# The opening of a one-core transformer kernel: loads by need, two tiles per pass, squares later, the norm by token

## The chip, the core and the metric

The kernel runs on one core of one Trainium2 chip. The metric is the device time of that core in microseconds (us). A core has TensorE (PE, matrix products into the eight banks of PSUM), VectorE (DVE), ScalarE (ACT), GpSimd (POOL), and SyncE (SP), which only issues transfers here. The engines run beside each other and wait for one another at semaphores; transfers run on 16 DMA engines, fed from the queues of SP, ACT and POOL.

## The reference, cut to what matters

The reference computes two transformer blocks over 512 tokens of width 1024: a recurrent layer with its feed-forward layer, an attention layer with its own, then a second block with retention, window attention and experts. The opening is the first norm and the first product of the recurrent layer:

```python
def rmsnorm(x, g):
    y = xf * lax.rsqrt(jnp.mean(xf * xf, axis=-1, keepdims=True) + EPS)
    return (y * g.astype(jnp.float32)).astype(x.dtype)

def rglru_mixer(h, w_in, conv_w, conv_b, ...):      # h is the normed input
    u = h @ w_in                                    # 1024 -> 2 x 1536
    xb, yb = u[..., :D_RNN], u[..., D_RNN:]
    y = jax.nn.gelu(yb)
    xc = conv over 4 tokens of xb, per channel, + conv_b
    r, i = sigmoid(gates of xc in blocks of 96)     # then a scan over the tokens
```

## The kernel before, in words

Activations lie turned: features on the 128 partitions, the 512 tokens along the free side. `h` holds x in eight tiles of 128 features (two tiles are one load, called x 0 to x 3 below). A product in full precision is made of three in a faster format: each operand is split into a high part (ScalarE rounds it: `a_hi`, `hn_hi`) and a rest (VectorE subtracts: `a_lo`, `hn_lo`), and `three` (L644 to L646) multiplies high by high, high by rest, rest by high. A tile of output is eight steps over the features, 24 matmuls. The norm's factor per token is applied behind the product, since it is the same for all features: the gain is multiplied into `hn_hi` and `hn_lo` at once, and VectorE multiplies the product by `rn`, the inverse root of the mean square, spread over all partitions.

Weights come as panels of 128 by 2048 (1 MB) into two buffers, `a_raw[0]` and `a_raw[1]`; each panel holds two tiles' weights for all eight steps, the two alternating step by step. Panels in the list `HALVES` are rounded in two halves of 1024 columns, so that a product can start with the first four steps.

The order of the work is written out by hand, for each engine:

- Transfers before: SP issues x 0 and panel 0, waits for x 2 (L562), and issues panels 1 to 3 as buffers come free. ACT's queue issues the first constants, x 1, x 2, x 3, the small tables `sm` and the other constants (L1521 to L1525).
- ScalarE before: rounds two tiles of x and squares them, twice; rounds panel 0 in halves; rounds the other four tiles, squaring one; rounds panel 1; takes the root (`root_wide`, L1512) of the sum; then the decay constants (Exp, Ln).
- GpSimd (L3079) adds squares 0 to 4 in four additions. VectorE makes squares 5 to 7, adds them, and adds GpSimd's sum (L2141): the sum of squares.
- TensorE before: 12 calls of `keep` (24 filler matmuls), then tile 0 of panel 0 over eight steps, tile 1 over five, `sums` (a product with a matrix of ones, which sums over the partitions and spreads the result over all of them, L734), the other three steps, and the two tiles of panel 1.
- VectorE before: after panel 1's rest the inverse of 128 by 512 numbers (L2117), then per group of three channel tiles: `take` (product times `rn`, L2207), `conv` (four taps, L2223 and L2226), `low_xc` (the rest of the convolved tile, L2234).
- `rnn_gates` (L792, L799, L800) multiplies the convolved tiles with the gates' weights, panel 2. It waits for the rests of tiles one and two, and later for the third. The gates' sigmoids, decays, the scan and the products of the next panels follow, in the same manner for four groups.

`token_sums` is there before and used in a late stage: it gives the sum of squares by token on the partitions, one column per 128 tokens, by a product whose moving side is one column.

Of the kernel before, what the change touches and what calls it, by code (L numbers as in the profile page):

```python
# [14 lines left out]
P = 128  # L15
# [95 lines left out]
HALVES = [A_RNN, A_K + 2, A_K + 4, A_K + 6, A_VCMP, A_W1V + 1, A_Q]  # L111
# [87 lines left out]
def build(nc, x_t, p_t, w_p, w_a, w_b, w_m, small, const, rope, decay, distance, out_t):  # L199
    ctx = ExitStack()  # L200
    with ctx:
# [331 lines left out]
        def _(sp):  # L533
# [25 lines left out]
            def load_x(i):  # L559
                sp.dma_start(h[:, 2 * i:2 * i + 2, :], x_t.rearrange("(k p) s -> p k s", p=P)[:, 2 * i:2 * i + 2, :]) \  # L560
                  .then_inc(x_loaded[i], 16)

            load_x(0)
            load_a(A_RNN)
            sp.wait_ge(x_loaded[2], 16)
            for u in range(1, 4):
                load_a(A_RNN + u)
# [68 lines left out]
        def _(pe):  # L636
# [99 lines left out]
            def token_sums(t):  # L736

                pe.wait_ge(sq_total, 3 * t + 3)
                for j in range(NT):
                    mm = pe.matmul(bank[4][:, j:j + 1], sq[:, 1, j * P:(j + 1) * P], ones[:, 0:1], start=True, stop=True)  # L740
                mm.then_inc(stat_mm, 1)
# [20 lines left out]
            def hh_first(k):  # L762
                rest(A_RNN, A_RNN, k)
                pe.wait_ge(hn_ready, KT * N_MIX0 + k + 1)
                return hh(k)

            def branch(g, panel, j, b, free, first=False):

                n = A_RNN + 4 * g + panel
                if j == 0:  # L770
                    whole(n, n)
                if g or panel == 3:
                    pe.wait_ge(tile_free, free)
                product(bank[b][:, :], n, j * P, 2 * P, P, hh_first if first else hh, hl).then_inc(tile_ready, 1)

            def rnn_gates(g):

                n = A_RNN + 4 * g + 2
                if g == 0:
                    keep(7, 3)  # L780
# [22 lines left out]
                pe.wait_ge(xc_ready, 3 * g + 2)  # L803
                for q in range(2):
                    own(0, q, True, False)
                pe.wait_ge(xb_taken, g + 1)
# [37 lines left out]
            keep(0, 12)  # L844
            for g in range(RNN_GROUPS):
                f = 8 * g - 3
                branch(g, 0, 0, 0, f, first=g == 0)
                if g:
                    branch(g, 0, 1, 1, f + 1)
                else:  # L850
                    product(bank[1][:, :], A_RNN, P, 2 * P, P, hh, hl, kt=5, last=False)
                    sums(T_MIX0, hs[:, 0, :])
                    product(bank[1][:, :], A_RNN, 5 * 2 * P + P, 2 * P, P, lambda k: hh(k + 5), lambda k: hl(k + 5), kt=3,
                            first=False).then_inc(tile_ready, 1)
                branch(g, 1, 0, 2, f + 2)
                branch(g, 1, 1, 3, f + 3)
                if g:
                    rnn_down(g - 1, 0, 4 if g < RNN_GROUPS - 1 else 2)
# [616 lines left out]
        def _(act):  # L1475
            step = Steps(act, act_step)

            def high_a(s, i=0):
# [4 lines left out]
                if s in HALVES:  # L1483
                    act.activation(a_hi[s % 2][:, 0:WB], a_raw[s % 2][:, 0:WB], ACT.Copy).then_inc(half_rounded, 1)
                    act.activation(a_hi[s % 2][:, WB:WA], a_raw[s % 2][:, WB:WA], ACT.Copy).then_inc(a_rounded, 1)
# [17 lines left out]
            def stat_wait(t):  # L1503
                act.wait_ge(stat_mm, t + 1 + (KT if t > T_KV else 0))
# [17 lines left out]
            for i in (1, 2, 3):  # L1522
                act.dma_start(h[:, 2 * i:2 * i + 2, :], x_v[:, 2 * i:2 * i + 2, :]).then_inc(x_loaded[i], 16)
            act.dma_start(sm[:, :], small).then_inc(params, 16)
            act.dma_start(cn[:, N_FIRST:N_CONST], const[:, N_FIRST:N_CONST]).then_inc(params, 16)  # L1525
            act.wait_ge(consts, 16)
            act.activation(warm[:, 0:1], eps, ACT.Sqrt)
            for i in range(2):
# [5 lines left out]
            high_a(A_RNN)  # L1534
            for m in range(4, KT):
                act.wait_ge(x_loaded[m // 2], 16)
                high_h(m, gain_of(0, m))
                if m == 4:
                    square(T_MIX0, m, h[:, m, :])
            high_a(A_RNN + 1)  # L1540
            root_wide(T_MIX0)


            act.wait_ge(params, 32)
# [3 lines left out]
            act.wait_ge(small_in, 1)  # L1548
            act.activation(spt[:, 3, :], spt[:, 2, :], ACT.Ln).then_inc(small_out, 1)
# [50 lines left out]
            for g in range(RNN_GROUPS + 1):  # L1600
# [23 lines left out]
                if g < RNN_GROUPS:  # L1624
                    high_xc(g, 0)
                    if g == 0:
                        high_a(A_RNN + 2)
# [99 lines left out]
            for m in range(KT):  # L1727
                if m < KT - 1:
                    act.wait_ge(stat_mm, T_KV + 1 + m + 1)
# [339 lines left out]
        def _(dve):  # L2069
            step = Steps(dve, dve_step)  # L2070
            V = dve

            def low_a(s, i=0):
                n = s + 2 * i
                if s in HALVES:
                    V.wait_ge(half_rounded, HALVES.index(s) + 1)
                    V.tensor_tensor(a_lo[s % 2][:, 0:WB], a_raw[s % 2][:, 0:WB], a_hi[s % 2][:, 0:WB], ALU.subtract) \  # L2077
                     .then_inc(half_ready, 1)
                    V.wait_ge(a_rounded, n + 1)
                    V.tensor_tensor(a_lo[s % 2][:, WB:WA], a_raw[s % 2][:, WB:WA], a_hi[s % 2][:, WB:WA], ALU.subtract) \  # L2080
                     .then_inc(a_ready, 1)
# [1330 lines left out]
```

## Time and profile before

| | |
|---|---|
| median of 3 runs | 2160.03 us (2158.39 to 2160.51) |
| the profiled execution | 2158.7 us, span 2156.9 us |
| PE busy | 2104.0 us, 98% of the span |
| DVE, ACT, POOL busy | 59%, 39%, 13% |
| granted PE clock, mean | 0.997 |

Times in the rows are from the start of the span. A row of the timeline gives start, duration, engine, line, operation, output and inputs, shape, how many operations were merged (x3), and in brackets the idle time just before it and what ended that. Matmuls overlap, so their starts tell more than their durations.

### The profile page before, as it was taken

The page shows a single profiled execution, that of the slowest core. Times are in us where ns is not written, and L with a number is a line of the kernel's source. Part 1 is how long each engine was busy: PE and PEld are TensorE (multiplying, and loading weights), DVE is VectorE, ACT ScalarE, POOL GpSimd, SP SyncE. Part 2 cuts the span into 40 slices and gives each one's busy share as a digit, 9 for nine tenths or more (in the row PEclk, how much of TensorE's full clock was granted, in tenths as well). Part 3 has the DMA queues.
Part 4 walks back from the last instruction along what each step waited for, and adds up shares of the span by engine and source line. Part 5 has one row for each costly group of instructions (what it writes and reads, how often), then busy time and mean ns, then how long its engine had stood idle before and what let it go on. Part 6 is the DMA issues. An engine that isn't in the chain of part 4 may idle for free.

```text
span 2156.9 us, 27242 instructions
## 1 busy us (share of the span) xinstructions
PE 2104.0 (98%) x10492; PEld 1583.7 (73%) x10492; DVE 1270.1 (59%) x1696; ACT 834.1 (39%) x1253; POOL 278.7 (13%) x238
## 2 busy tenths in 40 slices
PE   8999999999999999999999999999999999999998
PEld 6787788888878877888888888877778885333346
DVE  7877865555577678875655555577775454000038
ACT  5556522222253445774422222364542232222243
POOL 2334200000010064000100000020000023222220
PEclk9999999999999999999999999999999999999999
DMA  5322323223214352112332222121122158999951
GB/s 198 105 91 98 117 78 117 88 88 116 79 64 149 128 168 79 42 34 89 130 112 92 88 105 100 68 71 52 68 104 88 69 232 327 418 414 394 395 218 59
DMA packets 62478, 298.13 MB, mean 138 GB/s; under 512 B 14064, under 2 KB 14448, under 8 KB 34310
## 3 DMA queue, kind: packets, MB, share of 16 engines
q1 hardware_dynamic: 41584, 259.54, 31.5%
q0 software_dynamic: 19552, 34.55, 5.2%
q10 hardware_dynamic: 1248, 2.76, 0.3%
q8 instruction: 63, 1.03, 0.2%
q14 instruction: 31, 0.25, 0.0%
HBM read 326.37 MB, written 22.48 MB: 162 GB/s over the span
## 4 chain that ended last, share of the span: by engine, by line
PE 74%; DVE 13%; DMA 5%; ACT 4%; issue 3%; POOL 1%; ACTq 0%; DVEq 0%; POOLq 0%
PE psum L644 20%; PE psum L645 20%; PE psum L646 20%; PE psum L1390 4%; DMA panel<-w_m 4%; PE psum L1414 3%; PE psum L1084 2%; DVE a_lo L2085 2%; PE psum L1059 1%; DMA over_panel<-w_m,over_row 1%; ACT a_hi L1488 1%; DVE xc L2226 1%; DVE hs L2181 1%; ACT wp L1881 1%; DVE rn L2117 0%
## 5 line engine op out<-in xcount | busy, mean ns | idle before, releaser
L644 PE MATMUL psum<-hn_hi,a_hi 128*128 128x512 f32 (+1 forms) x1592 | 626.6, 394 | 4.9 <-DVE a_lo L2077 2.1
L646 PE MATMUL psum<-hn_hi,a_lo 128*128 128x512 f32 (+1 forms) x1592 | 619.1, 389 | 0.0
L645 PE MATMUL psum<-hn_lo,a_hi 128*128 128x512 f32 (+1 forms) x1592 | 618.8, 389 | 0.0
L644 PEld LDWEIGHTS psum<-hn_hi,a_hi 128*128 128x128 f32 (+1 forms) x1592 | 297.3, 187 | 77.3 <-issue 10.0
L646 PEld LDWEIGHTS psum<-hn_hi,a_lo 128*128 128x128 f32 (+1 forms) x1592 | 297.3, 187 | 64.4
L645 PEld LDWEIGHTS psum<-hn_lo,a_hi 128*128 128x128 f32 (+1 forms) x1592 | 297.3, 187 | 64.4 <-issue 2.2
L2085 DVE TENSOR_TENSOR a_lo<-a_raw,a_hi 128x2048 fp32r<-128x2048 f32 (+2 forms) x109 | 249.5, 2289 | 78.1 <-ACT a_hi L1488 77.6
L1488 ACT ACTIVATE a_hi<-a_raw 128x2048 fp32r<-128x2048 f32 (+2 forms) x109 | 203.2, 1866 | 73.2 <-PE psum L646 63.3
L2169 DVE TENSOR_TENSOR h<-h,psum 128x512 f32<-128x512 f32 x176 | 119.4, 687 | 78.4 <-PE psum L646 78.4
L3079 POOL TENSOR_TENSOR sq<-sq 128x512 f32<-128x512 f32 x6 | 9.0, 1504 | 1135.9 <-ACT sq L1501 1135.9
L3006 DVE TENSOR_TENSOR xhid<-xsg,psum 128x256 f32<-128x256 f32 x24 | 10.1, 421 | 232.4 <-ACT xsg L2035 232.4
L644 PE MATMUL psum<-hid_hi,b_hi 128*128 128x512 f32 x352 | 137.3, 390 | 2.2 <-DVE h L2169 2.1
L1658 ACT ACTIVATE sg<-sg 128x512 f32<-128x512 f32 x44 | 27.8, 632 | 286.3 <-DVE sg L2342 286.3
L646 PE MATMUL psum<-hid_hi,b_lo 128*128 128x512 f32 x352 | 137.0, 389 | 0.0
L645 PE MATMUL psum<-hid_lo,b_hi 128*128 128x512 f32 x352 | 137.0, 389 | 0.0
L1390 PE MATMUL psum<-panel,xw 128*64 128x512 f32 x512 | 113.4, 595 | 0.0
L2347 DVE TENSOR_TENSOR hid<-sg,psum 128x512 f32<-128x512 f32 x44 | 30.3, 688 | 113.8 <-PE psum L646 113.6
L1660 ACT ACTIVATE hid_hi<-hid 128x512 fp32r<-128x512 f32 x44 | 27.8, 632 | 177.5 <-DVE hid L2347 177.5
L1495 ACT ACTIVATE b_hi<-b_raw 128x1024 fp32r<-128x1024 f32 x64 | 66.9, 1050 | 59.2 <-PE psum L646 57.0
L1390 PEld LDWEIGHTS psum<-panel,xw 128*64 128x64 f32 x512 | 35.3, 137 | 66.8 <-issue 66.3
L2091 DVE TENSOR_TENSOR b_lo<-b_raw,b_hi 128x1024 fp32r<-128x1024 f32 x64 | 79.8, 1253 | 1.0 <-ACT b_hi L1495 1.0
L644 PEld LDWEIGHTS psum<-hid_hi,b_hi 128*128 128x128 f32 x352 | 66.1, 188 | 17.5 <-issue 2.6
(531 smaller groups left out, 3272.4 us busy)
## 6 DMA issues: line engine op xcount, KB each, us to landing
a_raw<-w_a SPq DMA_DIRECT2D x116, 1024.0 KB, 5.0
panel<-w_m SPq DMA_DIRECT2D x96, 1024.0 KB
b_raw<-w_b SPq DMA_DIRECT2D x64, 512.0 KB, 3.3
q_scratch<-q_hi POOLq DMA_DIRECT2D x7, 384.0 KB
q_scratch<-qb_lo POOLq DMA_DIRECT2D x7, 384.0 KB
q_hi<-q_scratch POOLq DMA_DIRECT2D x7, 384.0 KB
q_lo<-q_scratch POOLq DMA_DIRECT2D x7, 384.0 KB
token_rows<-nat POOLq DMA_DIRECT2D x4, 512.0 KB, 5.4
```

The source lines that it names most:

```text
L644: pe.matmul(out, w_hi, x_hi, start=first, stop=False)
L645: pe.matmul(out, w_hi, x_lo, start=False, stop=False)
L646: return pe.matmul(out, w_lo, x_hi, start=False, stop=last)
L1084: mm = pe.matmul(bank[6 + at % 2][side * DV:(side + 1) * DV, t * P:(t + 1) * P], w, x, start=i == 0, stop=i == len(steps) - 1)
L1390: mm = pe.matmul(bank[v][rows, :], xw[:, v, k, rows], w[half][:, k % 4 * 2 * EFF:(k % 4 + 1) * 2 * EFF], start=k == 0, stop=k == KT - 1)
L1414: mm = pe.matmul(bank[4 + 2 * v + hb][rows, :], xturn[:, v, f * P + half * SLOTS:f * P + (half + 1) * SLOTS], w[half][:, f * D + hb * 512: ...
L1488: act.activation(a_hi[s % 2][:, 0:w], a_raw[s % 2][:, 0:w], ACT.Copy).then_inc(a_rounded, 1)
L1495: act.activation(b_hi[s % 2][:, :], b_raw[s % 2][:, :], ACT.Copy).then_inc(b_rounded, 1)
L2085: V.tensor_tensor(a_lo[s % 2][:, 0:w], a_raw[s % 2][:, 0:w], a_hi[s % 2][:, 0:w], ALU.subtract) \
L2091: V.tensor_tensor(b_lo[s % 2][:, :], b_raw[s % 2][:, :], b_hi[s % 2][:, :], ALU.subtract) \
L2169: V.tensor_tensor(h[:, m, :], h[:, m, :], bank[4 + m % 4][:, :], ALU.add).then_inc(y_free, 1)
L2347: V.tensor_tensor(hid[:, f, :], sg[:, f, :], ps[1][:, :], ALU.mult).then_inc(tile_free, 2)
```

## The change

Transfers: panel 0 comes in two halves, the first of them as the first transfer of SP, then x 3 and panel 1; the small tables and the other constants move from ACT's queue to SP's, behind the first rounding; ACT's queue brings the first constants and x 0, x 1, x 2. TensorE makes both tiles of a panel in one pass over the eight steps (`first_tiles`), so that every step's input serves six matmuls at once; panel 1 is now also in `HALVES`. Squares 0 and 1 come after the second half of panel 0, squares 2 to 4 after the first half of panel 1. The norm is taken by token: `token_sums`, a root and an inverse of 128 by 4 numbers, four multiplications of the unit matrix by a column, and a product of ones with the resulting diagonal matrices, which spreads the factor over the partitions; ScalarE copies it to `rn`. Panel 2 is split before the first `take`. The fillers are six calls instead of 12, and the three before the gates go. In group 0 the second `take` comes before the first `low_xc`; in every group the third `take` comes before the second `low_xc`, and the own gates of the first tile wait for that tile alone.

```diff
+            sp.dma_start(a_raw[0][:, 0:WB], first[:, 0:WB]).then_inc(params, 16)
+            sp.dma_start(a_raw[0][:, WB:WA], first[:, WB:WA]).then_inc(a_loaded[0], 16)
+            sp.dma_start(h[:, 6:8, :], ...[:, 6:8, :]).then_inc(x_loaded[3], 16)
+            load_a(A_RNN + 1)
+            sp.wait_ge(half_rounded, 1)
+            sp.dma_start(sm[:, :], small).then_inc(params, 16)
+            sp.dma_start(cn[:, N_FIRST:N_CONST], const[:, N_FIRST:N_CONST]).then_inc(params, 16)
...
+            def first_tiles(panel):
+                s = A_RNN + panel
+                pe.wait_ge(half_ready, HALVES.index(s) + 1)
+                for k in range(KT):
+                    rest(s, s, k)
+                    if panel == 0:
+                        pe.wait_ge(hn_ready, KT * N_MIX0 + k + 1)
+                    for j in range(2):
+                        c = (2 * k + j) * P
+                        mm = three(bank[2 * panel + j][:, :], a_hi[s % 2][:, c:c + P], a_lo[s % 2][:, c:c + P],
+                                   hh(k), hl(k), k == 0, k == KT - 1)
+                        if k == KT - 1:
+                            mm.then_inc(tile_ready, 1)
+                        if panel and k == 2 and j == 0:
+                            pe.wait_ge(consts, 18)
+                            pe.matmul(bank[4][:, :], ones, hs[:, 1, :], start=True, stop=True).then_inc(stat_mm, 1)
+                    if panel and k == 0:
+                        token_sums(T_MIX0, hs[:, 0, :])
...
-            keep(0, 12)
+            keep(0, 6)
...
+            half_a(A_RNN, 0)                      # ScalarE
             for i in range(2):
                 act.wait_ge(x_loaded[i], 16)
                 for m in (2 * i, 2 * i + 1):
                     high_h(m, gain_of(0, m))
+            act.wait_ge(a_loaded[0], 16)
+            half_a(A_RNN, 1)
+            for m in range(2):
+                square(T_MIX0, m, h[:, m, :])
+            for i in range(2, 4):
+                act.wait_ge(x_loaded[i], 16)
                 for m in (2 * i, 2 * i + 1):
-                    square(T_MIX0, m, h[:, m, :])
...
+                    high_h(m, gain_of(0, m))
+            act.wait_ge(a_loaded[1], 16)
+            half_a(A_RNN + 1, 0)
+            for m in range(2, 5):
+                square(T_MIX0, m, h[:, m, :])
+            half_a(A_RNN + 1, 1)
+            root(T_MIX0)
+            high_a(A_RNN + 2)
+            act.wait_ge(stat_mm, 2)
+            act.activation(rn[:, :], bank[4][:, :], ACT.Copy).then_inc(small_out, 1)
...
             for m in range(5, KT):                # VectorE
                 step(V.tensor_tensor(hs[:, m - 5, :], h[:, m, :], h[:, m, :], ALU.mult))
+            half_a(A_RNN + 1, 0)
             for m in range(6, KT):
                 step(V.tensor_tensor(hs[:, 0, :], hs[:, 0, :], hs[:, m - 5, :], ALU.add))
             V.wait_ge(sq_summed, 4)
             V.tensor_tensor(hs[:, 0, :], hs[:, 0, :], sq[:, 0, :], ALU.add).then_inc(sq_total, 3)
-            low_a(A_RNN + 1)
-            inverse_wide(T_MIX0)
+            half_a(A_RNN + 1, 1)
+            inverse(T_MIX0)
+            V.wait_ge(dve_rstd, 1)
+            for j in range(NT):
+                spread = V.tensor_scalar(hs[:, 1, j * P:(j + 1) * P], ident, token[:, 1, j:j + 1], None, ALU.mult)
+            spread.then_inc(consts, 1)
+            low_a(A_RNN + 2)
```

## Rows read from the trace of the kernel before

**Rows 1.** The chain of waits over 0 to 50 us: start, duration, what.
```profile
1.25 7.65 DMA h<-x_t
45.36 0.70 DVE xc_lo L2234
```
**Rows 2.** Timeline of TensorE, from 13 to 97 us.
```profile
13.55 0.50 PE L644 MATMUL psum<-hn_hi,a_hi 128*128 128x512 f32 x1 [1.14 <-DVE a_lo L2077]
...
23.78 1.10 PE L734 MATMUL psum<-hs,cn 128*128 128x512 f32 x2
...
37.69 1.46 PE L640 MATMUL psum<-cn 128*128 128x256 f32 x6
...
46.11 0.49 PE L799 MATMUL psum<-xc_hi,a_hi 64*128 64x512 f32 x1 [0.65 <-DVE xc_lo L2234]
...
95.35 0.50 PE L644 MATMUL psum<-rhid_hi,b_hi 128*128 128x512 f32 x1 [1.99 <-DVE b_lo L2091]
```
**Rows 3.** Timeline of VectorE, from 23 to 40 us.
```profile
23.01 0.69 DVE L2141 TENSOR_TENSOR hs<-hs,sq 128x512 f32<-128x512 f32 x1
...
25.82 3.35 DVE L2117 RECIPROCAL rn<-rn 128x512 f32<-128x512 f32 x1
...
29.42 0.68 DVE L2207 TENSOR_TENSOR xb<-psum,rn 128x512 f32<-128x512 f32 x1
...
30.72 2.32 DVE L2226 SCALAR_TENSOR_TENSOR xc<-xb,sm,xc 128x511 f32<-128x511 f32 x3
...
37.90 2.02 DVE L2085 TENSOR_TENSOR a_lo<-a_raw,a_hi 128x1792 fp32r<-128x1792 f32 x1
```
**Rows 4.** Transfers: 0 to 4.5; 4.2 to 4.6; 4.5 to 7; 9 to 13; SP.
```profile
DMA packets 427, 0.82 MB, mean 183 GB/s; under 512 B 30, under 2 KB 158, under 8 KB 411
...
q1 hardware_dynamic: 53, 0.21, 125.8%
q10 hardware_dynamic: 3, 0.00, 1.2%
...
q1 hardware_dynamic: 108, 0.85, 83.2%
q10 hardware_dynamic: 89, 0.18, 18.8%
...
q10 hardware_dynamic: 650, 1.66, 105.0%
q1 hardware_dynamic: 1, 0.01, 1.4%
...
10.58 0.33 SPq L539 DMA_DIRECT2D a_raw<-w_a  x1
```
**Rows 5.** Timeline of ScalarE, from 8 to 13 us.
```profile
8.92 1.33 ACT L1515 ACTIVATE hn_hi<-h,cn 128x512 fp32r<-128x512 f32 x2 [1.16 <-DMA h<-x_t]
10.16 1.13 ACT L1501 ACTIVATE tmp<-h 128x512 f32<-128x512 f32 x2
11.20 1.04 ACT L1484 ACTIVATE a_hi<-a_raw 128x1024 fp32r<-128x1024 f32 x1
```
**Rows 6.** Timeline of GpSimd and VectorE, from 7 to 16 us.
```profile
7.85 1.26 POOL L3079 TENSOR_TENSOR sq<-sq 128x512 f32<-128x512 f32 x1 [7.38 <-ACT sq L1501]
12.27 1.23 DVE L2077 TENSOR_TENSOR a_lo<-a_raw,a_hi 128x1024 fp32r<-128x1024 f32 x1 [1.18 <-ACT a_hi L1484]
12.36 2.28 POOL L3079 TENSOR_TENSOR sq<-sq,tmp 128x512 f32<-128x512 f32 x1
13.41 2.32 DVE L2080 TENSOR_TENSOR a_lo<-a_raw,a_hi 128x1024 fp32r<-128x1024 f32 x1
```
**Rows 7.** Token sums in a later stage (timeline); narrow multiplications (groups: count, total, mean ns).
```profile
1766.40 0.95 PE L740 MATMUL psum<-cn,sq 128*128 128x1 f32 x8
...
L2684 DVE TENSOR_SCALAR wp<-wp,wst 128x128 f32<-128x128 f32 x8 | 2.2, 281 | 0.0
```
**Rows 8.** TensorE near 1470 us: timeline, and busy times with the granted clock (PEclk).
```profile
1468.92 1.09 PE L1185 MATMUL psum<-cn,wp 128*128 128x128 f32 x8 [3.02 <-DVE wp L2684]
...
1470.00:1472.00 2.00, 2.00 (x7) 1.57 (x6) 2.00 (x3) 1.93 (x2) 0.00 (x0) 0.53 0.00 0
```

More of the change, by code:

```diff
@@ L759, in down, with branch @@
                                 mm.then_inc(y_ready, 1)
[L762 to L767, printed above, removed]
+            def first_tiles(panel):
[16 more added lines that the diff above has]
+                        token_sums(T_MIX0, hs[:, 0, :])
+            def branch(g, panel, j, b, free):
                 n = A_RNN + 4 * g + panel
@@ L771, in branch @@
                     whole(n, n)
-                if g or panel == 3:
-                    pe.wait_ge(tile_free, free)
-                product(bank[b][:, :], n, j * P, 2 * P, P, hh_first if first else hh, hl).then_inc(tile_ready, 1)
+                pe.wait_ge(tile_free, free)
+                product(bank[b][:, :], n, j * P, 2 * P, P, hh, hl).then_inc(tile_ready, 1)
             def rnn_gates(g):
                 n = A_RNN + 4 * g + 2
-                if g == 0:
-                    keep(7, 3)
                 pe.wait_ge(a_ready, n + 1)
@@ L843, in _ @@
             pe.wait_ge(consts, 16)
-            keep(0, 12)
+            keep(0, 6)
             for g in range(RNN_GROUPS):
                 f = 8 * g - 3
-                branch(g, 0, 0, 0, f, first=g == 0)
                 if g:
+                    branch(g, 0, 0, 0, f)
                     branch(g, 0, 1, 1, f + 1)
-                else:
[L851 to L858, printed above, removed]
+                    branch(g, 1, 0, 2, f + 2)
+                    branch(g, 1, 1, 3, f + 3)
+                    rnn_down(g - 1, 0, 4 if g < RNN_GROUPS - 1 else 2)
+                else:
+                    first_tiles(0)
+                    first_tiles(1)
                 if 0 < g < RNN_GROUPS - 1:
@@ L1476, in _, with half_a @@
             step = Steps(act, act_step)
+            def half_a(s, half):
+                c = slice(WB * half, WB * half + WB)
+                act.activation(a_hi[s % 2][:, c], a_raw[s % 2][:, c], ACT.Copy) \
+                   .then_inc(a_rounded if half else half_rounded, 1)
             def high_a(s, i=0):
@@ L1521, in _ @@
             act.dma_start(cn[:, 0:N_FIRST], const[:, 0:N_FIRST]).then_inc(consts, 16)
-            for i in (1, 2, 3):
+            for i in range(3):
                 act.dma_start(h[:, 2 * i:2 * i + 2, :], x_v[:, 2 * i:2 * i + 2, :]).then_inc(x_loaded[i], 16)
-            act.dma_start(sm[:, :], small).then_inc(params, 16)
-            act.dma_start(cn[:, N_FIRST:N_CONST], const[:, N_FIRST:N_CONST]).then_inc(params, 16)
             act.wait_ge(consts, 16)
             act.activation(warm[:, 0:1], eps, ACT.Sqrt)
+            act.wait_ge(params, 16)
+            half_a(A_RNN, 0)
             for i in range(2):
@@ L1531, in _ @@
                     high_h(m, gain_of(0, m))
-                for m in (2 * i, 2 * i + 1):
-                    square(T_MIX0, m, h[:, m, :])
[L1534 to L1544, printed above, removed]
+            act.wait_ge(a_loaded[0], 16)
[4 more added lines that the diff above has]
+                act.wait_ge(x_loaded[i], 16)
+                for m in (2 * i, 2 * i + 1):
+                    high_h(m, gain_of(0, m))
[8 more added lines that the diff above has]
+            act.activation(rn[:, :], bank[4][:, :], ACT.Copy).then_inc(small_out, 1)
+            act.wait_ge(params, 48)
             lam = smc("lam", 0, RNN_TILES)
@@ L2071, in _, with half_a @@
             V = dve
+            def half_a(s, half):
+                c = slice(WB * half, WB * half + WB)
+                if half:
+                    V.wait_ge(a_rounded, s + 1)
+                else:
+                    V.wait_ge(half_rounded, HALVES.index(s) + 1)
+                V.tensor_tensor(a_lo[s % 2][:, c], a_raw[s % 2][:, c], a_hi[s % 2][:, c], ALU.subtract) \
+                 .then_inc(a_ready if half else half_ready, 1)
             def low_a(s, i=0):
@@ L2215, in conv @@
                 if t < 2:
-                    take(g, t)
+                    if n != 1:
+                        take(g, t)
                 else:
@@ L2270, in _ @@
                     conv(g, 0)
+                    if g == 0:
+                        one_more()
+                        take(0, 1)
                 if 0 < g < RNN_GROUPS:
```

68 lines of the change are left out of this document (30 added, 38 removed).

## The prediction

> **What bounds the kernel now.** I read the busy table first: the matrix engine is busy for 98% of the span. Then the waits of that engine, to see where the rest goes, and the chain of waits over the first 75 us, to see which of the opening's waits set the end. The reader is to see three things. The first product starts at 13.55 and the four tiles of the opening end at 37.7, where the filler matmuls begin [rows 2]. The gate products then wait twice for VectorE's xc_lo, the second time until 46.11 [rows 1, 2]. And behind 46.11 the products run until a wait of 1.99 at 95.35, again for VectorE [rows 2]; that chain starts at the gates, since their sigmoids wait for TensorE. So the opening is worth what it brings forward one event, the third xc_lo, which ends at 46.05 (45.36 + 0.69), and all behind it moves with it one for one. Before it lies one unbroken VectorE chain from the sum of squares (23.01 + 0.69 = 23.7): half of a panel's rounding rest, the wide reciprocal 3.35, the take at 29.42, three convolutions with a panel's rest 2.02 between them [rows 3].
>
> That fixes the method: find the end of the sum of squares after the change, add the new way to the take, add the new way to the third xc_lo, and compare with 46.05.
>
> **From the take to the third xc_lo.** Now 46.05 - 29.42 = 16.63. The rest of panel 2 (2.02, L2085) moves ahead of the take. The 0.70 in which VectorE waits for ScalarE's first xc_hi is now filled: the log's addition (0.17, moved) and the second take (0.7) stand there. Sum 16.63 - 2.02 - 0.70 + 0.2 = 14.1. The sample is 3.62 for the first convolution (29.42 to 30.72 + 2.32) [rows 3]. Taking the third tile ahead of low_xc costs nothing: its 0.6 covers the second rounding. The table load for Exp and the one for Ln lie beside convolutions, where ScalarE waits for VectorE. PE's first own gates no longer wait for the second xc_lo, but they are not last: the third is.
>
> **From the sum to the take.** Now 29.42 - 23.7 = 5.7: panel 1's rest 2.1, the wide reciprocal 3.35, two small operations. After: four matmuls by one column, 0.95 [rows 7]; root, high part of panel 2 (1792 wide, about 1.7 by the 1.04 of 1024 [rows 5]) and its rest 2.02, masks 0.15; with the gaps, 5.15. Beside it on TensorE: 0.95, six and three products at 0.23 = 2.05, the spreading product 1.10 [rows 2], the copy 0.7: 4.8, so both ways are about equally long and neither hides much of the other. VectorE's own part (half a rest 1.2, a reciprocal of four columns, four 128-wide multiplies) ends before TensorE reaches the spreading product. The 3.35 is thus mostly paid again: gain 0.55. Behind the waiting spreading product stand 33 products of panel 1 (7.5), due for the third take some 8 us later: no loss.
>
> So the third xc_lo ends at (end of the sum) + 5.15 + 14.1 = sum + 19.25, and the change wins only if the sum ends before 46.05 - 19.25 = 26.8. It could be 3.1 us later than now. The rest is: when does it end?
>
> **Arrivals.** The queues (q1 is SP's, q10 ACT's) have moved 0.82 MB at 4.5 us and then 0.40 MB per us [rows 4]. Two orders are possible when both queues hold work. In order of issue: from 4.2 to 4.6 the SP queue moved 53 packets and the ACT queue 3, though slice 1 of x had been issued there at 1.25 [rows 1, 4], and from 9 to 13 the SP queue moved 1 packet, though panel 1 was issued at 10.58, until the ACT queue was nearly empty [rows 4]. Packet by packet in turn: from 4.5 to 7 it was 108 packets to 89 [rows 4]; these two had been issued together. I take issue order, with turns within a pair issued together. Check on now: constants 0.17, x 0 0.52, panel 0 1.05, x 1 0.52 are 2.27 MB, moved at 8.1; its landing was 8.9 [rows 1, 5], so about 0.75 is added.
> After, pairs as issued: (half panel 0, constants) 0.70 MB, landed 5.0; (other half, x 0) 1.75 MB, 6.8 + 0.75 = 7.5; (x 3, x 1) 2.8 MB, 10.3; (panel 1, x 2) 4.36 MB, 13.4 + 0.75 = 14.1. The small tables follow behind, by 17, and are needed at 31.
> The Trainium skill's DMA: Bandwidth & Descriptors (Queues, rings and completion order) says that an engine takes the queues in turn, packet by packet; by that alone x 1 would land at 12.8 instead of 10.3; it is rival D, which is worked out from the rows.
>
> **ScalarE** (rounding 0.66, square 0.56, half panel 1.0 [rows 5]): half panel from 5.5; x 0 rounded 7.5 to 8.85; x 1 10.3 to 11.65; second half to 12.6; two squares to 13.65; x 2 and x 3 14.1 to 16.6; half of panel 1 to 17.6; squares 2 to 4 end at 18.1, 18.7, 19.2.
> TensorE starts at 9.0 (7.5, a rounding 0.66, a rest 0.7; now 13.55), four steps of 1.37 with hardly a wait to 14.5, waits for x 2 until 15.7, and ends both tiles at 21.2. That is the gain the change is built on: 4.5 us at its start.
>
> **VectorE and GpSimd** decide. GpSimd adds squares: 1.26 with VectorE idle, 2.28 beside a rest of VectorE, whose next rest took 2.32 for 1.23 [rows 6]. Each waits for the other to end: a GpSimd addition holds VectorE up by about 1.1. Now these pairs lie at 12 to 17, before the sum's chain; after, three additions fall into the middle of it, because squares 2 to 4 come last. VectorE: rests of x end at 17.6, then three squares (0.7), the half rest of panel 1 (1.15), two additions (0.7), final addition 0.7, and between them three additions of GpSimd at 1.15: 17.6 + 2.1 + 1.15 + 1.4 + 0.7 + 3.45 = 26.4. Half of panel 1 is ready only at 24.3, so TensorE idles 21.2 to 24.3.
> The Trainium skill's SBUF — State Buffer (SBUF: two separate sides) calls it an exclusive lock on a port pair that the two engines share, taken for a whole operation; this trace agrees with 2.28 and 2.32. It speaks against the change, and by it the sum is at 26.4.
> Without such waits VectorE's own work to 22.6 and GpSimd's three additions, 1.26 each from 18.1 on with what they lose, would let the sum end near 24.1: a rival.
>
> **Sum.** Take at 26.4 + 5.15 = 31.55, third xc_lo at 45.65, against 46.05: 0.4 us gained. The profiled execution took 2158.7 (span 2156.9), so 2158.3 for such a one; the median of the runs, 2160.03, stands 1.3 above it, and I forecast 2160.0 - 0.4 = 2159.6. Removed fillers (six and three calls) stood in idle time and cost nothing.
>
> **Unknown costs and bounds.** The lock: 0 to 3 x 1.1; I take 2.3 net (26.4 against 24.1), nearest to the pair in rows 6. Four diagonal multiplies, not in the trace: the nearest, 128 wide, took 0.28 each [rows 7], so 0 to 1.1 in all; VectorE has 1.3 to spare there, so hidden at either end. x 2: 11.6 (panel 1 held back as from 9 to 13) to 16.6 (below, D); at 11.6 ScalarE's own work becomes the limit and 0.45 is all that is won.
>
> **Rivals.**
> (B) No lock where it matters: the additions of GpSimd fall into VectorE's gaps. Sum 24.1, change 24.1 + 19.25 - 46.05 = -2.7: 2157.3. For it: the first addition took 1.26. Against: VectorE has no gap after 17.6.
> (C) Slower, by TensorE's clock. Place: the idle 21.2 to 24.3. After a wait of 3.02 at 1468.92 the granted clock was 0.53 (the lower level, 1.2 GHz) from 1470 to 1472 [rows 8]. Price: the nine products between the sum and the spreading product take 0.43 instead of 0.23, 1.8 more, and the spreading product up to 1; the path there has 0.35 to spare: +2.5 - 0.4 = +2.1: 2162.1. It decides from a wait near 3 us on; against it, 1.99 at 95.35 [rows 2] did no harm.
> (D) Slower, by turns: a packet of the one queue, then one of the other, as 108 to 89 [rows 4]. Packets are rows: 4 KB of a half panel, 2 KB of x, 8 KB of panel 1. The halves overtake x 0 (landed 8.1), and x 1's last packet moves with panel 1's last, at 3.84 MB, so 12.05 + 0.75 = 12.8. ScalarE reaches squares 2 to 4 at 20.2 to 21.3, the sum ends at 28.3: +1.5: 2161.5. Were the small tables to take turns with x 2 as well, x 2 would land with them, at 5.36 MB: 16.6, which costs 0.4 more, since ScalarE is ready for it at 16.2.
> (E) Much faster: x lands early and no lock, sum near 22.2: -4.6: 2155.4. It needs two of my readings wrong.
>
> **Chances.** Forecast 0.40, B 0.21, C 0.12, D 0.12, E 0.15. A measurement of this kernel tells 0.2% (4.3 us) from nothing. Beyond -4.3 lies E, and not all of it is deeper: 0.13 faster. Beyond +4.3 lie only C and D together, 0.06. So 0.81 within. The range takes in B, C, D and the edge of E: 2155.5 to 2162.8.
>
> **What would show it.** First product near 9 and not 13.5; both tiles of panel 0 ended near 21; a wait of 2 to 3 us before panel 1; GpSimd's last three additions at 1.8 to 2.3 each, between 18 and 23; the sum at 26.4; the copy of the norm at about 31; third xc_lo at 45.6. A granted clock below 1 near 24 would be C; x 1 after 12, D. The forecast fails if the sum ends before 25, or if the first convolution starts before 29.4, and also if the gates' gain is not found again at the wait now at 95.35.

## The result, and the profile after

The changed kernel takes 2163.83 us (median of 21 runs, 2160.96 to 2164.96), the kernel before 2160.01 (21 runs beside them, 2158.37 to 2161.13): a ratio of 1.0017, 95% interval 1.0011 to 1.0023. It is 3.8 us slower; forecast were 0.4 us faster and a range that ended at 2162.8. The profiled execution took 2164.38 us (span 2162.6, mean granted clock 0.996).

TensorE's timeline of the changed kernel:

```profile
15.43 0.50 PE L645 MATMUL psum<-hn_hi,a_hi 128*128 128x512 f32 x1 [1.37 <-DVE hn_lo L2157]
19.26 0.47 PE L645 MATMUL psum<-hn_hi,a_hi 128*128 128x512 f32 x1 [0.81 <-DVE hn_lo L2157]
27.47 0.50 PE L645 MATMUL psum<-hn_hi,a_hi 128*128 128x512 f32 x1 [2.49 <-DVE a_lo L2106]
29.70 1.75 PE L741 MATMUL psum<-cn,hs 128*128 128x1 f32 x8
35.13 1.02 PE L779 MATMUL psum<-hs,cn 128*128 128x512 f32 x2
51.17 0.49 PE L812 MATMUL psum<-xc_hi,a_hi 64*128 64x512 f32 x1 [1.55 <-DVE xc_lo L2277]
...
100.61 0.50 PE L645 MATMUL psum<-rhid_hi,b_hi 128*128 128x512 f32 x1 [1.99 <-DVE b_lo L2123]
```

Set these beside [rows 2]. The last two lines answer to the waits at 46.11 and 95.35: 5.06 and 5.26 later. So the opening's loss is carried on almost one for one, as the method said, and nearly everything is decided before the third xc_lo: the two profiled executions, 2164.38 and 2158.7, differ by 5.7, more than the medians do. Against the kernel before, which waited once for the rests of x, for 1.00, TensorE now waits twice for them, and new is the wait of 2.49 ahead of panel 1.

VectorE's timeline:

```profile
18.31 2.79 DVE L2157 SCALAR_TENSOR_TENSOR hn_lo<-h,cn,hn_hi 128x512 fp32r<-128x512 f32 x4 [0.90 <-ACT hn_hi L1532]
21.02 4.19 DVE L2170 TENSOR_TENSOR hs<-h 128x512 f32<-128x512 f32 x3
25.25 2.17 DVE L2106 TENSOR_TENSOR a_lo<-a_raw,a_hi 128x1024 fp32r<-128x1024 f32 x1
27.34 1.41 DVE L2173 TENSOR_TENSOR hs<-hs 128x512 f32<-128x512 f32 x2
28.83 0.69 DVE L2175 TENSOR_TENSOR hs<-hs,sq 128x512 f32<-128x512 f32 x1
...
31.78 0.18 DVE L2145 RECIPROCAL token<-token 128x4 f32<-128x4 f32 x1 [1.12 <-ACT token L1525]
32.00 0.87 DVE L2181 TENSOR_SCALAR hs<-cn,token 128x128 f32<-128x128 f32 x4
33.37 2.03 DVE L2117 TENSOR_TENSOR a_lo<-a_raw,a_hi 128x1792 fp32r<-128x1792 f32 x1 [0.50 <-ACT a_hi L1505]
36.82 0.23 DVE L2186 CAST masks<-cn 128x128 bf16<-128x128 f32 x1 [1.42 <-ACT rn L1567]
36.96 0.68 DVE L2249 TENSOR_TENSOR xb<-psum,rn 128x512 f32<-128x512 f32 x1
...
50.42 0.69 DVE L2277 TENSOR_TENSOR xc_lo<-xc,xc_hi 128x512 fp32r<-128x512 f32 x1 [0.69 <-ACT xc_hi L1624]
```

The sum of squares ends at 29.52 (28.83 + 0.69); in [rows 3] it was 23.7, forecast were 26.4. The take is at 36.96, 7.44 after it, where 5.15 were forecast. The third xc_lo ends at 51.11, 14.15 after the take, where 14.1 were forecast.

ScalarE's timeline (its waits date the arrivals) and GpSimd's:

```profile
9.25 1.34 ACT L1532 ACTIVATE hn_hi<-h,cn 128x512 fp32r<-128x512 f32 x2 [2.13 <-DMA h<-x_t]
13.87 1.33 ACT L1532 ACTIVATE hn_hi<-h,cn 128x512 fp32r<-128x512 f32 x2 [3.28 <-DMA h<-x_t]
17.55 2.56 ACT L1532 ACTIVATE hn_hi<-h,cn 128x512 fp32r<-128x512 f32 x4 [0.36 <-DMA h<-x_t]
21.66 2.99 POOL L3120 TENSOR_TENSOR sq<-sq,tmp 128x512 f32<-128x512 f32 x2 [3.10 <-ACT tmp L1518]
24.80 1.53 POOL L3120 TENSOR_TENSOR sq<-sq,rstd 128x512 f32<-128x512 f32 x1
```

x 0, x 1 and x 2 arrived at 9.25, 13.87 and 17.55; forecast were 7.5, 10.3 and 14.1. Next, transfers in 0 to 5 us, then by queue in 10 to 11 and 13 to 14 us (packets, MB, share of the engines):

```profile
DMA packets 277, 0.75 MB, mean 151 GB/s; under 512 B 17, under 2 KB 130, under 8 KB 277
...
q1 hardware_dynamic: 39, 0.32, 77.0%
q10 hardware_dynamic: 40, 0.08, 21.8%
...
q1 hardware_dynamic: 78, 0.25, 63.3%
q10 hardware_dynamic: 81, 0.15, 39.8%
```

From 10 to 11 panel 1 (q1, rows of 8 KB) and x 1 (q10, rows of 2 KB) move one packet each in turn, so x gets 0.08 MB per us and panel 1 gets 0.32, though x 1 was issued first. From 13 to 14 the small tables (q1, rows of about 3.3 KB) do the same to x 2. The Trainium skill's DMA: Bandwidth & Descriptors (Queues, rings and completion order) says that each engine takes the queues in turn, a packet at a time; the trace agrees, 39 to 40, where one packet in the profile is one row.

Last, busy times and granted clock (third number from the end) from 26 to 38 us:

```profile
26.00:28.00 2.00, 0.53 (x2) 0.48 (x3) 2.00 (x2) 0.00 (x0) 0.33 (x1) 1.00 0.00 0
28.00:30.00 2.00, 2.00 (x7) 1.36 (x7) 1.88 (x4) 0.00 (x0) 0.00 (x0) 0.52 0.00 0
30.00:32.00 2.00, 2.00 (x9) 1.90 (x10) 0.84 (x3) 0.51 (x2) 0.00 (x0) 0.50 0.43 70
32.00:34.00 2.00, 2.00 (x6) 1.54 (x5) 1.50 (x5) 1.33 (x1) 0.00 (x0) 0.50 0.76 299
34.00:36.00 2.00, 2.00 (x7) 1.27 (x6) 1.40 (x1) 0.00 (x0) 0.00 (x0) 0.77 0.99 408
36.00:38.00 2.00, 2.00 (x10) 1.64 (x9) 1.15 (x3) 1.79 (x3) 0.00 (x0) 1.00 1.06 401
```

After the wait of 2.49 the granted clock is at its lower level (1.2 of 2.4 GHz) until about 35. Exactly there stand the token sums (1.75 us instead of 0.95 [rows 7]) and the products up to the spreading one. Two causes, then, sum up to the 5.06: a sum that is late by 3.1 against the forecast, and 2.3 more between the sum and the take; with the forecast of -0.4 that makes 5.0.

### The profile page after: what moved, and what is told of

It reads as the page before. It is cut to its first block, busy times and chain, and to the rows that moved or that the text cites. A ratio compares the mean times of both kernels' runs of the same rounds, so it can differ in the third digit from the quotient of the medians.

```text
span 2162.6 us, 27236 instructions
## 1 busy us (share of the span) xinstructions
PE 2105.2 (97%) x10482; PEld 1583.1 (73%) x10482; DVE 1269.3 (59%) x1701; ACT 834.6 (39%) x1255; POOL 277.5 (13%) x238
## 3 DMA queue, kind: packets, MB, share of 16 engines
q10 hardware_dynamic: 960, 1.75, 0.2%
## 4 chain that ended last, share of the span: by engine, by line
PE 74%; DVE 12%; DMA 6%; ACT 4%; issue 3%; POOL 1%; ACTq 0%; DVEq 0%; POOLq 0%
PE psum L645 20%; PE psum L646 20%; PE psum L647 20%; PE psum L1401 5%; PE psum L1425 3%; DMA panel<-w_m 3%; PE psum L1095 2%; DVE a_lo L2117 1%; PE psum L1070 1%; DMA over_panel<-w_m,over_row 1%; ACT a_hi L1505 1%; DVE xc L2269 1%; DMA h<-x_t 1%; DVE hs L2223 1%; ACT wp L1907 1%
```

## The experiments

Each kernel was timed in 5 rounds beside the kernel before (medians of that: 2160.23 in the first group of four runs, 2159.22 in the second, 2159.41 in the last three). e1 to e5 are the changed kernel with one edit, e6 is e1 with one, e8 to e11 are e7 with one; where an edit moves arrivals, ScalarE and VectorE follow the new order. "Sum" is the end of the sum of squares, "take" the start of the first take and "third xc_lo" the end of that operation, all in the profiled execution; the kernel before has 23.7, 29.42 and 46.05. "Against before" is the difference of the medians. The ratio is not formed from the medians: for e1 it is 1.0014, by the medians it would be 1.0008.

| kernel | sum | take | third xc_lo | against 46.05 | median | against before | ratio, 95% interval |
|---|---|---|---|---|---|---|---|
| changed kernel | 29.5 | 36.96 | 51.11 | +5.1 | 2163.83 | +3.8 | 1.0011 to 1.0023 |
| e1 fillers | 29.5 | 34.65 | 48.81 | +2.8 | 2161.89 | +1.7 | 1.0005 to 1.0023 |
| e2 panel 1 held | 26.9 | 32.77 | 46.92 | +0.9 | 2160.93 | +0.7 | 0.9997 to 1.0015 |
| e3 squares early | 28.7 | 33.90 | 48.06 | +2.0 | 2161.58 | +1.4 | 0.9999 to 1.0017 |
| e4 old transfers | 25.9 | 32.38 | 46.54 | +0.5 | 2160.41 | +0.2 | 0.9994 to 1.0012 |
| e5 VectorE adds | 28.7 | 35.27 | 49.40 | +3.4 | 2163.12 | +3.9 | 1.0008 to 1.0026 |
| e6 e1, wide norm | 29.8 | 37.35 | 51.50 | +5.5 | 2164.98 | +5.8 | 1.0015 to 1.0034 |
| e7 winner | 21.1 | 26.99 | 41.13 | -4.9 | 2154.64 | -4.6 | 0.9965 to 0.9983 |
| e8 e7, GpSimd adds | 20.9 | 26.77 | 40.92 | -5.1 | 2153.64 | -5.6 | 0.9960 to 0.9982 |
| e9 e7, new transfers | 25.6 | 31.44 | 45.59 | -0.5 | 2158.67 | -0.7 | 0.9988 to 1.0006 |
| e10 e7, panel 0 halved | 21.0 | 26.81 | 40.96 | -5.1 | 2153.91 | -5.5 | 0.9961 to 0.9983 |
| e11 e7, wide norm | 20.2 | 28.38 | 42.51 | -3.5 | 2155.37 | -4.0 | 0.9972 to 0.9990 |

In all twelve the take is followed by the third xc_lo's end after 14.13 to 14.16 us, and the fifth column and the seventh differ by at most 1.3 us. Read from one execution each, this event ranks the kernels as the medians do, but for e5 and the changed kernel, which change places. Where the two columns part, a conclusion below goes no further than what both say.

**e1: fillers before panel 1** (does the clock cost 2.3?).

```diff
                 s = A_RNN + panel
+                if panel:
+                    keep(5, 6)
                 pe.wait_ge(half_ready, HALVES.index(s) + 1)
```

> The changed kernel with six filler calls put where TensorE waits for panel 1's first half (24.98 to 27.47 in its trace). Theory C (the wait, 2.5 us behind two shorter ones, lets the clock fall, and the products between the sum and the spreading product run at half speed): the granted clock stays at 1.00 from 28 to 36, the token sums take 0.95 and not 1.75, the copy of the norm starts near 34.0 instead of 36.19, the third xc_lo ends near 48.9 instead of 51.1, and the time is 2.0 to 2.3 below the changed kernel's median of 2163.8, so near 2161.6; single runs scatter less than its 2161.0 to 2165.0. Rival (the low clock has another cause, or is not on the path): clock and times as they are, 2163.8.

The granted clock was 1.00 in every slice from 20 to 36, and at the same sum (29.54) the take came 2.3 earlier. The two lines of TensorE, token sums and spreading product:

```profile
29.59 1.05 PE L741 MATMUL psum<-cn,hs 128*128 128x1 f32 x8 [0.45 <-DVE hs L2177]
32.66 1.02 PE L781 MATMUL psum<-hs,cn 128*128 128x512 f32 x2
```

From token sums to spreading product it was 3.07 us instead of 5.43. So theory C is shown, and its size on the path, 2.3, by one trace of each kernel. The times bear it out less sharply: the medians differ by 1.9 (2163.83 and 2161.89), but the intervals of the two ratios overlap.

**e2: panel 1 held until x 2 has landed** (are the turns the delay?).

```diff
+            sp.wait_ge(x_loaded[2], 16)
             load_a(A_RNN + 1)
```

> The changed kernel, but SP issues panel 1 and all behind it only when x 2 has landed. Theory T (the two queues are served in turn, packet by packet, so the 8 KB rows of panel 1 take four fifths of the bytes from x 1 and x 2): x 1 lands near 10.9 instead of 13.8, x 2 near 12.1 instead of 17.5, panel 1 near 17; the sum of squares ends near 26 instead of 29.5, third xc_lo 3 to 3.5 earlier, 2160.3 to 2160.8. Rival (order of issue, as I had forecast, with only a slow start): x 1 and x 2 land within 0.5 of where they do now and the time stays 2163.8 or is worse by panel 1's delay.

ScalarE's timeline:

```profile
9.49 1.33 ACT L1533 ACTIVATE hn_hi<-h,cn 128x512 fp32r<-128x512 f32 x2 [2.28 <-DMA h<-x_t]
11.26 1.34 ACT L1533 ACTIVATE hn_hi<-h,cn 128x512 fp32r<-128x512 f32 x2 [0.43 <-DMA h<-x_t]
...
14.49 2.55 ACT L1533 ACTIVATE hn_hi<-h,cn 128x512 fp32r<-128x512 f32 x4
17.35 1.06 ACT L1493 ACTIVATE a_hi<-a_raw 128x1024 fp32r<-128x1024 f32 x1 [0.32 <-DMA a_raw<-w_a]
```

x 1 comes 2.6 earlier; x 2 is there by 12.50, when SP issues panel 1, 5 us earlier, and is no longer waited for. The sum ends at 26.85, 2.7 earlier. That is the price of rival D's turns, those with the small tables included, since they stand behind panel 1 in SP's queue and are held as well; and it is most of the 3.1 by which the sum missed. x 0 is as late as without the hold (9.49). The clock falls here too (0.50 from 26 to 28, after a wait of 2.45), but costs only 0.8 against e1, since it is back at 1 before the spreading product. So the third xc_lo comes 4.2 earlier, 2.7 by the sum and 1.5 by the clock.

**e3: the squares in the order of before** (does the lock go?). ScalarE squares 0 to 3 between its first roundings and 4 after the rounding of tile 4.

> The changed kernel with the squares where they were before (0 to 3 behind their roundings, 4 behind the fifth). Theory S (squares 2 to 4 come last and GpSimd's three additions lie between VectorE's operations, 3.1 us of waits, and hold both the sum and panel 1's half back): VectorE's three squares take 2.1 and not 4.2, the half rest 1.2 and not 2.2, the sum ends near 26.5 instead of 29.5, third xc_lo 3 earlier, 2160.8; and the wait before panel 1 shrinks under 1, so the clock may hold, 2.3 more: 2158.5. Rival (VectorE is bound by the arrival of x 2 alone): the sum moves by less than 1, 2163 or more.

```profile
18.52 4.78 DVE L2156 SCALAR_TENSOR_TENSOR hn_lo<-h,cn,hn_hi 128x512 fp32r<-128x512 f32 x4
23.23 2.13 DVE L2169 TENSOR_TENSOR hs<-h 128x512 f32<-128x512 f32 x3
25.39 1.22 DVE L2105 TENSOR_TENSOR a_lo<-a_raw,a_hi 128x1024 fp32r<-128x1024 f32 x1
```

A miss: I expected the sum at 26.5 and it was 28.7. The squares take 2.13 and the half rest 1.22 again, but now the four rests take 4.78 instead of 2.79: the additions fall there. Moving the squares only moves the lock; with x this late both orders put the additions beside VectorE's work. The take still came 3.1 earlier, by the clock: it fell earlier (0.50 from 22 to 24), was back at 1.00 from 26 on, before the token sums, and from sum to take it was 5.17 instead of 7.44.

**e4: the transfers of before**, with ScalarE and VectorE in that order of arrival; all else as changed.

> The changed kernel with the loads of the kernel before (x 0 first on SP, then panel 0 as one load, panel 1 behind x 2; x 1 to x 3 and the tables on ACT's queue); ScalarE rounds x 0 first and then panel 0's first half. Theory T: x 0 lands at 5.3, x 1 at 8.9, x 2 near 10.5; first product near 10.5; the last rests of x end near 17 instead of 21.1, the sum near 24 to 25, and the time is 4.5 to 5.5 below the changed kernel: 2158.3 to 2159.3 (2 more if the clock holds). Rival (loads matter little, the squares and the lock decide): the sum stays within 1.5 of 29.5, 2162 or more.

The sum moved 3.6 earlier, to 25.94, but not to 24 or 25: the lock now fell on the half rest (2.21 instead of 1.22) and on VectorE's two additions (3.45 instead of 1.41), 3.0 us again. TensorE then waited 2.03 at the token sums and its clock was 0.59 and 0.55 from 28 to 32. The transfers are the larger part of the loss, but the time was above the range that I expected; with them alone undone the change is worth nothing (+0.2).

**e5: VectorE makes the additions** (the lock by itself).

```diff
+            def add_square(k):
+                V.wait_ge(sq_ready, k + 1)
+                step(V.tensor_tensor(sq[:, 0, :], sq[:, 0, :], SQUARES[k], ALU.add))
...
+            add_square(1)                         # behind panel 0's second rest
...
-            V.wait_ge(sq_summed, 4)
+            for k in range(2, 5):                 # behind VectorE's own two additions
+                add_square(k)
...
-            sums(T_MIX0)                          # GpSimd
```

> The changed kernel with one thing changed: the four additions of squares 0 to 4 are made by VectorE (0.69 each) instead of GpSimd; GpSimd has no work in the opening. In the changed kernel VectorE's three squares took 4.19 us and half a rest 2.17, where three squares took 2.13 and half a rest 1.22 when GpSimd stood still. Theory of the lock (while GpSimd works, VectorE stands): the squares take 2.13 and the half rest 1.2 again, panel 1's first half is ready 3 us earlier (27.4 to about 24.4), TensorE's wait before panel 1 goes from 2.49 to under 0.5, its granted clock stays at 1, and the sum, with three more additions on VectorE, ends at 21.0 + 2.13 + 1.2 + 1.4 + 3 x 0.69 + 0.69 = 28.5 instead of 29.5; third xc_lo 48.8 less 1.0 = 47.8, time 3.3 us under the changed kernel's: about 2160.6. Rival: VectorE's operations were slow there for another reason (the transfers that write the same memory meanwhile, 0.4 MB per us); then the squares stay near 4, the sum is at 30.5 or later, and nothing is won.

VectorE's timeline, against 4.19 and 2.17 above:

```profile
21.02 2.13 DVE L2176 TENSOR_TENSOR hs<-h 128x512 f32<-128x512 f32 x3
23.20 1.23 DVE L2106 TENSOR_TENSOR a_lo<-a_raw,a_hi 128x1024 fp32r<-128x1024 f32 x1
```

The same operations at the same time, with GpSimd still: 2.06 and 0.94 less. The lock is shown (the Trainium skill's SBUF — State Buffer (SBUF: two separate sides) has a pair of ports that VectorE and GpSimd share and that one of them holds for a whole operation while the other is blocked, and 2.13 against 4.19 agrees). Its net price is small, 0.8 at the sum, as VectorE now has the additions itself. TensorE's wait before panel 1 went, but it stood 2.43 at the token sums instead, and the clock fell there (0.57 from 30 to 34). The clock's loss that I had expected to vanish only moved; the median gained 0.7 at most, not 3.3.

**e6 and e11: the wide norm again**, in e1 and in e7: `sums`, `root_wide`, `inverse_wide` for the token sums, the small root and inverse, the diagonals, the spreading product and the copy.

> The changed kernel with the fillers before panel 1 (as in the run before that kept TensorE's clock at 1: sum 29.54, take 34.65, third xc_lo ends 48.81), and with the norm as it was before the change: the wide sum, root and inverse of 128 by 512 numbers in place of the token sums and the spreading product; panel 2's rest stays ahead of the take. By the theory that the norm by token is what pays for panel 2's rest: sum 29.5, product with ones and root 1.9, inverse 3.35, rest 2.02, masks and gaps 0.3: take at 37.1, 2.4 later than with the token norm, third xc_lo 51.2, time 2.4 us above that run. Rival, as my prediction had it (the 3.35 is mostly paid again by the token way): take at most 0.6 later.

> The version that beat both (third xc_lo ends 41.13, median 2154.6) with the wide norm of the kernel before in place of the token sums and the spreading product, all else the same. Sum at 21.1, product with ones and root until 23.1, inverse 3.35 to 26.5 (beside it nothing else on VectorE), panel 2's rest 2.02, masks and gaps 0.3: take at 28.8 to 29.3 instead of 27.0, third xc_lo 43.0 to 43.4, time 1.9 to 2.3 us above: 2156.7. Rival (mostly paid again by the token way, as I predicted): at most 0.6 us above.

The wide norm of e11, its product with ones on TensorE and its inverse on VectorE:

```profile
21.02 1.02 PE L731 MATMUL psum<-hs,cn 128*128 128x512 f32 x2
22.79 3.35 DVE L2146 RECIPROCAL rn<-rn 128x512 f32<-128x512 f32 x1 [0.27 <-ACT rn L1522]
```

From sum to take it is 5.11 in e1 and 7.52 in e6: the norm by token saves 2.4 there, once panel 2's rest stands in that stretch. In e7 and e11 the sum is over before TensorE comes to use it (21.11 and 20.25, used at 21.31 and 21.02), so the stretch is counted from there: 5.68 and 7.36, a saving of 1.7; the take itself is 1.4 later in e11. The times agree in direction: the median of e6 lies 3.1 above e1's, that of e11 0.7 above e7's (by the ratios 2.4 and 1.5; the intervals overlap in both pairs). "Mostly paid again", a gain of 0.55, was too dark: the token way leaves VectorE free for the panel's rest, the wide inverse (3.35) does not. This part of the change is good.

**e7 and e8: a version meant to beat both.**

```diff
-            half_a(A_RNN, 0)                      # ScalarE, against the changed kernel
             for i in range(2):
                 act.wait_ge(x_loaded[i], 16)
                 for m in (2 * i, 2 * i + 1):
                     high_h(m, gain_of(0, m))
-            act.wait_ge(a_loaded[0], 16)
+                if i == 0:
+                    for m in range(2):
+                        square(T_MIX0, m, h[:, m, :])
+                    act.wait_ge(a_loaded[0], 16)
+                    half_a(A_RNN, 0)
             half_a(A_RNN, 1)
-            for m in range(2):
+            for m in range(2, 4):
                 square(T_MIX0, m, h[:, m, :])
...
+            square(T_MIX0, 4, h[:, 4, :])
+            act.activation(hs[:, 0, :], h[:, 5, :], ACT.Square).then_inc(sq_ready, 1)
             act.wait_ge(a_loaded[1], 16)
             half_a(A_RNN + 1, 0)
-            for m in range(2, 5):
-                square(T_MIX0, m, h[:, m, :])
+            for m in range(6, KT):
+                act.activation(hs[:, m - 5, :], h[:, m, :], ACT.Square).then_inc(sq_ready, 1)
...
+                        if panel == 0 and k == KT - 1 and j == 0:      # TensorE
+                            token_sums(T_MIX0, hs[:, 0, :])
+                        if panel and k == 0 and j:
                             pe.wait_ge(consts, 18)
```

and the transfers of before. e7 makes the additions on VectorE, e8 on GpSimd.

> A version meant to beat both: the transfers of the kernel before (x 0, whole panel 0, panel 1 only after x 2), the two tiles per pass, the norm by token and the order behind it from the change; ScalarE makes all eight squares, 0 and 1 before panel 0 has landed, 2 to 5 between the roundings, 6 and 7 behind panel 1's first half; VectorE makes all seven additions (GpSimd none) ahead of panel 1's rest; the token sums stand in panel 0's last step, the spreading product behind panel 1's first step. Theory (lock gone, arrivals as in the run with these transfers, panel 0 at 9.0, x 3 by 15, panel 1 at 17.4): rests of x end at 16.7, additions to 20.9 (sum; kernel before 23.7), TensorE's panel 0 ends near 23 without a wait of over 1 us, spread at 24.7, take at 27.2, third xc_lo ends at 41.5 to 42 instead of 46.05: 4.3 us under the kernel before, 2155.9. Rival: TensorE's own time becomes the bound (four tiles cannot end before 35.4, the third take then waits): third xc_lo 43 or later, 2157 or above.

> The same version with GpSimd's four additions kept (VectorE adds squares 5 to 7 and the rest). Theory of the lock: three of the four additions fall between VectorE's rests and cost it 1.1 each: four rests of x take 5 to 6 us where they take 2.8, sum at 22.1 or later, 1.2 us after the version without them; time 1.2 us above it. Rival: GpSimd's additions are free help: the sum ends 1.5 us earlier, since VectorE has four additions (2.8 us) less.

TensorE of e7:

```profile
10.97 0.50 PE L641 MATMUL psum<-hn_hi,a_hi 128*128 128x512 f32 x1 [1.66 <-DVE a_lo L2108]
21.31 0.94 PE L737 MATMUL psum<-cn,hs 128*128 128x1 f32 x8
24.43 1.13 PE L777 MATMUL psum<-hs,cn 128*128 128x512 f32 x2
41.19 0.49 PE L808 MATMUL psum<-xc_hi,a_hi 64*128 64x512 f32 x1 [1.55 <-DVE xc_lo L2288]
90.42 0.50 PE L641 MATMUL psum<-rhid_hi,b_hi 128*128 128x512 f32 x1 [1.98 <-DVE b_lo L2125]
```

After the first product TensorE waits for nothing until the third xc_lo, and the clock is 1.00 in every slice from 20 to 54. Both versions beat both kernels, by 0.26% and 0.29% against the kernel before. In e8 four rests of x took 5.63 us instead of 2.74 (the lock, where I had put it): VectorE lost 2.9 and was spared four additions of 0.69. Its sum ended at 20.94 instead of 21.11; I had expected it 1.2 later. But in e7 the sum did not follow VectorE alone. Panel 1 arrived at 17.95 there, in e8 at 16.74, and squares 6 and 7, which ScalarE makes behind its first half, held VectorE up by 0.66. In e11 VectorE has the same work up to the sum and panel 1 arrived at 17.09; its sum ended at 20.25. So who adds makes between 0.2 us for GpSimd and 0.7 against it, not 1.2, and the medians of e7 and e8 (intervals overlapping) do not tell the two apart.

**e9: e7 with the changed kernel's transfers.**

> The version with all squares on ScalarE and all additions on VectorE, but with the changed kernel's transfers (half panel 0 first, x 3 and panel 1 beside x 1 and x 2). With the old transfers that version had its first product at 10.97, the sum at 21.11, the third xc_lo's end at 41.13 and a median of 2154.6. Theory (the turns of the two queues are what the change's transfers cost): x 1 again at 13.9 and x 2 at 17.5, TensorE waits 1.4 and 0.8 for them, panel 0 ends at 24 to 25 instead of 23.2, the rests of x at 20.9, sum 24.0 or a little earlier, take 28.5 to 29, third xc_lo 43.0: 1.9 us above that version, about 2156.5, still under the kernel before. Rival: with the squares placed well the arrivals do not matter any more, since TensorE starts as early as there and catches up: within 0.5 us of it.

x arrived at 9.65, 14.16 and 17.81; TensorE waited 1.43 and 0.71 for it and 1.14 for the sum (25.60). Third xc_lo 4.5 later than in e7, more than the 1.9 expected: the last rests of x start at 18.57, and behind them stand six additions in a row. So with these squares too the transfers alone undo almost all that the other parts can win: 4.5 of 4.9 by the event, and by the medians all but 0.7.

**e10: e7 with panel 0 in two transfers behind x 0**, squares 6 and 7 ahead of panel 1.

> The version that beat both, with panel 0 in two transfers of 1024 columns behind x 0 on SP's queue (the small tables after the first rounding, behind panel 1) and squares 6 and 7 ahead of panel 1's rounding. Theory: the first half of the panel lands 2 us before the whole did (8.5), the first product starts at 9.2 to 9.5 instead of 10.97, the sum ends at 20 instead of 21.1; the third take must wait for TensorE's last tiles of panel 1 (34 or so, now just done at 35), so only about 0.7 to 1.5 us is won: third xc_lo 39.7 to 40.4, time 2153.2 to 2154. Rival: rows of 4 KB start slower, as in the changed kernel, where only 0.75 MB had been moved at 5 us against 1.05 MB before and the constants landed 1.2 us later; then x 1 and panel 1 land over 1 us later as well, TensorE waits for them and nothing is won.

The half panel was there at 7.77, the whole one in e7 at 8.53; the first product started at 10.14 instead of 10.97, but the take came only 0.2 earlier. ScalarE may round panel 2 only when panel 0's tiles are done (22.99, in e7 23.18), and that with panel 2's rest is what the take now follows. The medians (2153.91 against 2154.64, intervals overlapping) tell no difference. The constants landed at 4.75 here, so half panels behind x 0 do not slow the start.

## Why the prediction was wrong

Right were the method and three of its terms: the event that decides (third xc_lo; all kernels of the table follow it), take to third xc_lo (14.1, measured 14.15), the lock in the sum's chain (forecast 1.15 for each of three additions, 3.45; measured 2.06 + 0.94, 3.0 us, while the additions themselves took 1.5 each and not 1.8 to 2.3), and the panel's half rest as what TensorE waits for (a wait of 2 to 3 us; 2.49).

The step that failed is "I take issue order, with turns within a pair issued together". Both readings were open in [rows 4], and the two rows that I took for issue order do not show it. The row of 4.2 to 4.6 (53 packets to 3) is a short pause of the ACT queue between the constants and x 1, in which it moved 4 packets until 4.8. Ahead of it, from 2.8 to 4, the two queues had gone in turn with the constants and x 0:

```profile
q1 hardware_dynamic: 138, 0.28, 60.8%
q10 hardware_dynamic: 129, 0.16, 40.7%
```

The other row is the wait of a new transfer. From 9 to 13 the SP queue moved 1 packet though panel 1 had been issued at 10.58, behind three slices of x that had waited in the other queue since 1.25. In e7, e8 and e11, with the same transfers, its first packet again moved 2.1 to 2.8 us after its issue, while the ACT queue was full. In e2 it was issued at 12.50, onto idle engines, and its first packet moved after 13.4: about 0.9 us of the delay is there without any other traffic. The rest of that row, and the pause, no run here explains; but both concern the start of a transfer, and the changed kernel issues panel 1 at 2.15, so both queues are full when x 1's turn comes. For that, 108 to 89 was the row to go by. I had worked D out (x 1 at 12.8, x 2 at 16.6, the sum at 28.3 and with the small tables up to 0.4 more) and gave it 0.12. Measured were 13.9, 17.6 and 29.5; e2 puts the turns at 2.7 us of the sum.

What D lacked is the slow start: 0.75 MB at 5 us against 1.05 MB before, constants at 5.97 against 4.78, and everything behind them a microsecond later. In all seven kernels with the changed transfers TensorE's first use of the constants was between 5.96 and 6.31, in the five with the old ones between 4.80 and 5.59, in e10 at 4.75. The arrangement does it, but why stays open: e10 excludes the half panel as such, not the half panel ahead of x 0.

The second step that failed is the 5.15 from sum to take, in which the clock stood at nothing; it measured 7.44. Its mechanism (idle before panel 1, clock at the lower level for the products between the sum and the spreading one) and its price (+2.5 on the path; e1 measures 2.3) stood in the prediction; against it I set that 1.99 at 95.35 did no harm, and gave it 0.12. The forecast itself had TensorE idle for 3.1 us there, the length of the one wait in [rows 8] behind which the clock had been 0.53. By its own rows C was the likelier case.

So C and D came together, with the slow start on top; I had given that case 0.06 at most (beyond +4.3), and the median's +3.8 lies just short of it. C did not need D: in e2, with x 1 and x 2 earlier, TensorE still waited 2.45 and the clock fell behind it, but it cost 0.8 there and not 2.3.

Smaller: TensorE's start at 9.0 came at 10.9, because x 0 was there at 9.25, forecast 7.5; D, with its turns against the halves, has 8.1, and the slow start is the likely rest. "Neither hides much of the other" of the two ways from sum to take was right at full clock: 5.11 in e1, forecast 5.15.

## What to carry to other kernels

Before a transfer is moved earlier, ask with whom it will share the engines: a queue with long rows beside one with short rows takes the bandwidth in proportion to the rows, here 4 to 1, and the early panel was paid for with 2.7 us at the sum of squares. Where a forecast contains an idle stretch of TensorE ahead of products on the critical path, price the lower clock into it, and put fillers there; here two lines brought the take 2.3 us forward and the median 1.9. A change of many parts is best judged by one event that all its parts move: here the end of one operation at 46 us told the medians of twelve kernels to within 1.3 us.

## What was not expected of the hardware

The length of a wait alone does not say whether the clock falls. It fell behind waits of 2.49, 2.45, 2.43 and 2.03 and, in e3, in the slices behind waits of 1.36 and 1.83:

```profile
20.00:22.00 2.00, 1.58 (x6) 1.13 (x6) 2.00 (x3) 2.00 (x4) 1.43 (x1) 0.87 0.76 311
22.00:24.00 2.00, 2.00 (x6) 1.59 (x6) 1.97 (x4) 0.60 (x1) 0.00 (x0) 0.50 0.35 147
24.00:26.00 2.00, 2.00 (x9) 1.59 (x8) 1.93 (x3) 0.00 (x0) 0.00 (x0) 0.78 0.00 0
```

In e11 it stayed at 1.00 behind this one:

```profile
37.77 0.50 PE L805 MATMUL psum<-xc_hi,a_hi 64*128 64x512 f32 x1 [2.49 <-DVE xc_lo L2279]
```

in e6, behind waits of 2.08 and 2.48 at 42.64 and 46.75, and in e9, behind waits of 1.43, 0.71 and 1.14, it stayed as well. What tells these apart the runs do not show.
